# Four residual gemms with rows of tokens out of PSUM, and norms that run one token tile after another

## What is computed

```python
# first block
xn = rms_norm(h, ln1_w); proj = xn @ w_in                      # 1024 -> IN_WIDTH
mix = concat(nsa_mixer(...), retention_mixer(...))
h = h + mix @ w_out                                            # 1024 x 1024
hn = rms_norm(h, ln2_w)
h = h + square(relu(hn @ w_up)) @ w_down                       # 1024 -> 4096 -> 1024
# second block
sh1, sc1, g1, sh2, sc2, g2 = split(silu(c) @ w_ada + b_ada, 6)
hh = standardize(x) * (1 + sc1) + sh1
mix = hybrid_mixer(hh, ...)            # mLSTM and S5, ends in y @ w_mix_out (1024 x 1024)
x = layer_norm(ALPHA * x + (1 + g1) * mix, ln1_gain, ln1_bias)
hh = standardize(x) * (1 + sc2) + sh2
f = conv_glu_ffn(hh, ...)              # 1024 -> 2 x 2816, 2816 -> 1024
x = layer_norm(ALPHA * x + (1 + g2) * f, ln2_gain, ln2_bias)
```

## Time and profile before

| what | us |
|---|---|
| median of the timed runs (3) | 1843.65 (1843.37 to 1845.13) |
| profiled execution, its own time | 1839.39 |
| span of the profiled execution, first to last instruction | 1837.5 |
| PE busy | 1576.4 (86%) |
| DVE busy | 1116.4 (61%) |
| POOL busy | 638.7 (35%) |
| ACT busy | 580.2 (32%) |

### The profile page before, as it was taken

One profiled execution on the slowest core, in us unless ns is written; L12 is line 12 of the kernel. 1 busy time (PEld: TensorE's weight loads), 2 busy tenths in 40 slices (PEclk: granted clock), 3 DMA queues, 4 the chain that ended last, 5 costly groups with the idle time before them and its releaser, 6 DMA issues. The chain is left out here.

```text
span 1837.5 us, 19435 instructions
## 1 busy us (share of the span) xinstructions
PE 1576.4 (86%) x6984; PEld 1225.2 (67%) x6984; DVE 1116.4 (61%) x1935; ACT 580.2 (32%) x779; POOL 638.7 (35%) x456
## 2 busy tenths in 40 slices
PE   3999776788999998979998887566996699999995
PEld 3778534576878777868765554344885588888874
DVE  5743467735777977446899999864644532232236
ACT  3333255214322222233222311354332333333331
POOL 2344000023545554533434241101554244445442
PEclk9999679989999999999999988778998799999998
DMA  6221100042555453222322211122330223222221
GB/s 255 89 74 67 45 1 1 1 176 79 198 173 191 163 195 137 92 92 70 108 97 75 103 69 57 52 78 69 140 115 24 92 99 108 92 92 93 92 90 46
DMA packets 37303, 178.76 MB, mean 97 GB/s; under 512 B 4192, under 2 KB 5088, under 8 KB 22496
## 3 DMA queue, kind: packets, MB, share of 16 engines
q1 hardware_dynamic: 31968, 168.15, 26.3%
q10 hardware_dynamic: 5248, 9.44, 1.4%
HBM read 166.04 MB, written 10.49 MB: 96 GB/s over the span
## 5 line engine op out<-in xcount | busy, mean ns | idle before, releaser
L1132 POOL TENSOR_TENSOR wlo<-raw,whi 128x512 fp32r<-128x512 f32 x336 | 466.2, 1414 | 1157.2 <-ACT whi L753 1157.2
L409 PE MATMUL bank<-Ahi,whi 128*128 128x512 f32 x1152 | 473.8, 411 | 7.9 <-POOL wlo L1134 7.1
L411 PE MATMUL bank<-Ahi,wlo 128*128 128x512 f32 x1152 | 452.5, 393 | 0.0
L410 PE MATMUL bank<-Alo,whi 128*128 128x512 f32 x1152 | 452.3, 393 | 0.0
L409 PEld LDWEIGHTS bank<-Ahi,whi 128*128 128x128 f32 x1152 | 219.2, 190 | 68.2 <-issue 21.6
L410 PEld LDWEIGHTS bank<-Alo,whi 128*128 128x128 f32 x1152 | 218.8, 190 | 54.3 <-issue 10.9
L411 PEld LDWEIGHTS bank<-Ahi,wlo 128*128 128x128 f32 x1152 | 218.3, 189 | 46.7
L409 PE MATMUL bank<-Bhi,whi 128*128 128x512 f32 x560 | 222.9, 398 | 9.3 <-POOL wlo L1134 5.6
L753 ACT ACTIVATE whi<-raw 128x2048 fp32r<-128x2048 f32 x112 | 214.2, 1913 | 52.5 <-DMA raw<-in_ws 44.6
L410 PE MATMUL bank<-Blo,whi 128*128 128x512 f32 x560 | 219.9, 393 | 0.0
L411 PE MATMUL bank<-Bhi,wlo 128*128 128x512 f32 x560 | 219.9, 393 | 0.0
(11 more groups left out here) (366 smaller groups left out, 2047.5 us busy)
## 6 DMA issues: line engine op xcount, KB each, us to landing
raw<-in_ws SPq DMA_DIRECT2D x112, 1024.0 KB, 5.1
adaw<-in_ada SPq DMA_DIRECT2D x48, 512.0 KB, 4.4
spill<-stage ACTq DMA_DIRECT2D x32, 256.0 KB, 2.0
X<-in_x SPq DMA_DIRECT2D x8, 512.0 KB, 5.3
gates<-spill SPq DMA_DIRECT2D x16, 256.0 KB, 5.4
w1k<-in_w1k SPq DMA_DIRECT2D x1, 2048.0 KB, 16.3
w1v<-in_w1v SPq DMA_DIRECT2D x1, 2048.0 KB, 20.5
XM<-spill SPq DMA_DIRECT2D x8, 256.0 KB, 2.9
```

The lines of the kernel that those rows point to most:

```text
L409: pe.matmul(ps[:], wh, hi[:, k], start=(k == 0), stop=False)
L410: pe.matmul(ps[:], wh, lo[:, k], start=False, stop=False)
L411: ins = pe.matmul(ps[:], wl, hi[:, k], start=False, stop=(k == kn - 1))
L1132: pool.tensor_tensor(wlo[slot][:, part], raw[slot][:, part], rd(whi[slot][:, part]), ALU.subtract)
```

## The change

The gemms `wout`, `dn`, `mix` and `fd` now hold the activation tile as the stationary operand and stream 512 weight columns (`token_gemm`). A bank then has 128 tokens by 512 features. Half 0 of the features is made in four T banks, half 1 in G, G, O, O. The number of matmuls stays (192 for 8 feature tiles). Where a norm follows, half 1 runs in the order (part 0, tile 0), (0,1), (0,2), (1,0), (0,3), (1,1), (1,2), then tile 0's transposes (`wout` and `dn3`), then (1,3). DVE adds a bank to `X` directly; ACT copies, sums in `Y` and PE's turns back are gone. For `mix` and `fd` the gain lies along the free dimension: `widen` and `spread` make `G1b` and `G2b` by transposing matmuls, and the addition is two DVE operations.

All norms run tile by tile: root and row scaling on ACT (whole 1024-wide rows of all tiles), then the turned tile is scaled by 8 ACT operations of 128 columns (`scaled`), and DVE splits it (`parts`) after the statistics of the tile behind it. `layer_norm`'s gain and bias are on DVE for all tiles; POOL only makes `wlo`.

Two chunks of zeros (`pad0` after WIN, `pad1` after `if`) make 113 tiles, and move the tile borders: `up0.0` and `up0.1` now share tile 16 (before `up0.0` was the end of tile 15, `up0.1` and `up0.2` tile 16, and so on), `wout.0.0` is the first half of tile 12 (before `wout0` was the end of tile 11). The ada tiles are used one after each `up` chunk of groups 0 to 2, six after the last of them and two between the halves of `dn` (before one after each `up` and `dn` chunk), and the S5 pieces are regrouped. The second load of `GB`, and the weight tiles behind it, now wait for all of the middle LayerNorm.

```diff
     for g, kg in enumerate(FF1_GROUPS):
-        ch += [(f"up{g}.{j}", 8) for j in range(kg)] + [(f"dn{g}.{n}", kg) for n in range(DC)]
-    ch += [(f"us{c}", 8) for c in range(4)] + [("if", 8)]
+        ch += [(f"up{g}.{j}", 8) for j in range(kg)] + token_chunks(f"dn{g}", kg)
+    ch += [(f"us{c}", 8) for c in range(4)] + [("if", 8), ("pad1", 8)]
...
+                def products(ps, q, ks, half, i, k, stop):
+                    b = FIRST_BLOCK[g + 2 * half + q] + 4 * (k - ks[0])
+                    t, c = b // TILE_BLOCKS, b % TILE_BLOCKS
+                    wh, wl = (w[t % 2][:, c * P:(c + 4) * P] for w in (whi, wlo))
+                    h, l = (x[:, k, i * P:(i + 1) * P] for x in (hi, lo))
+                    pe.matmul(ps[:], h, wh, start=(k == 0), stop=False)
+                    pe.matmul(ps[:], h, wl, start=False, stop=False)
+                    return pe.matmul(ps[:], l, wh, start=False, stop=stop)
...
+                    for q, i in ((0, 0), (0, 1), (0, 2), (1, 0), (0, 3), (1, 1), (1, 2)):
+                        run(q, i)
+                    if turns:
+                        normed_tile(s, 0)
+                    run(1, 3)
...
+            def normed_out(s, more=None):
+
+                for i in range(NT + 1):
+                    if i < NT:
+                        root(i, s)
+                        normed_row(i, s)
+                    if i == 1 and more is not None:
+                        hi_upto(more)
+                    if i == 1 and s == 2:
+                        act.wait_ge(sem("mod_ready"), A.due("mod_ready"))
+                    if i:
+                        scaled(i - 1, s)
...
+            def add_token(name, half, i, gain=None, alpha=None):
+
+                n = f"{name}.{half}t{i}"
+                dve.wait_ge(*full(n))
+                ps = bank_of(n)
+                x = X[:, i, half * S:(half + 1) * S]
+                if gain is None:
+                    tt(x, x, ps[:], ALU.add).then_inc(taken(n)[0], 1)
+                    dve.wait_ge(*taken(n))
                 else:
...
+                    t = G8[2]
+                    tt(t[:], ps[:], gain[:, half * S:(half + 1) * S], ALU.mult).then_inc(taken(n)[0], 1)
...
+            def rows_of(name, s):
+
+                for i in range(NT):
+                    add_token(name, 0, i)
+                    half_stats(i, 0)
+                for i in range(NT):
+                    add_token(name, 1, i)
+                    half_stats(i, 1)
+                    row_stats(i, s < 2)
+                    row_scale(i, s < 2)
+                    if i:
+                        parts(s, i - 1)
+                parts(s, NT - 1)
...
                     dve.sem_inc(sem("up_used"), 1)
+                    if g < 3:
+                        ada_tile()
+                if g < 3:
+                    for _ in range(6):
+                        ada_tile()
...
+                for i in range(NT):
+                    add_token(f"dn{g}", 0, i)
+                for _ in range(2):
                     ada_tile()
...
+            for i in range(NT):
+                add_token("mix", 1, i, G1b, ALPHA)
+                half_stats(i, 1)
+                row_stats(i, False)
+                row_scale(i, False)
+                gained(i)
+                half_stats(i, 0)
+                half_stats(i, 1)
+                row_stats(i, False)
+                row_scale(i, False)
+                if i:
+                    parts(3, i - 1)
+            dve.sem_inc(sem("gb_used"), 1)
+            parts(3, NT - 1)
```

More of the change, by code:

```diff
@@ L67, in plan_chunks @@
         ch += [(f"gv{n}", 4), (f"gg{n}", 4), (f"md{n}", 8)]
-    ch += [(f"mix{n}", 8) for n in range(DC)]
+    ch += token_chunks("mix", 8)
     for g, kg in enumerate(FF2_GROUPS):
@@ L428, in _, with spread @@
+            def spread(name, c):
+                pe.wait_ge(sem("mod_wide"), T.due("mod_wide"))
+                ps, where = bank("T")
+                for n in range(4):
+                    ins = pe.matmul(ps[:, n * P:(n + 1) * P], Fb[c % 2][:, n * P:(n + 1) * P], ident, start=True,
+                                    stop=True)
+                done(ins, f"{name}.{c}", where)
             pe.wait_ge(sem("con_in"), T.due("con_in", 16))
-            normed_in(0)
+            for i in range(NT):
+                normed_tile(0, i)
@@ L582, in _ @@
                     done(ins, f"ry{h - 1}", where)
[L585 to L600, removed]
+            token_gemm("wout", Bhi, Blo, 8, "B_ready", True, 1)
             for g, kg in enumerate(FF1_GROUPS):
@@ L802, in _, with plain_rows, through @@
+            def plain_rows(i):
+                root(i, 2)
+                act.wait_ge(sem("rstd_ready"), A.due("rstd_ready"))
+                act.activation(X[:, i, :], X[:, i, :], ACT.Identity, scale=sd[:, i:i + 1],
+                               bias=nmr[:, i:i + 1]).then_inc(sem("ln_rows"), 1)
+            def through(name):
+                for half in range(2):
+                    for q in range(2):
+                        hi_upto(last_tile(INDEX[f"{name}.{half}.{q}"]))
             act.wait_ge(sem("con_in"), A.due("con_in", 16))
@@ L926, in _ @@
                 act.wait_ge(sem("sd_ready"), A.did("sd_ready"))
-            def back_out(name, buf, scale=1.0, wait=None):
-                ps = take(name)
-                if wait is not None:
-                    act.wait_ge(*full(wait))
-                act.activation(buf, ps[:], ACT.Copy, scale=scale).then_inc(taken(name)[0], 1)
-            for n in range(DC):
-                back_out(f"wout{n}", G4[n % 4][:], wait=f"wout{n - 4}T" if n >= 4 else None)
-            sqrt_sd()
-            normed_out(1)
+            through("wout")
+            normed_out(1, last_tile(INDEX["wout.1.1"]) + 1)
             act.wait_ge(sem("cB_in"), A.due("cB_in", 16))
@@ L1093, in _ @@
             act.wait_ge(sem("g8_free"), A.due("g8_free"))
-            for n in range(DC):
-                back_out(f"mix{n}", G8[n % 2][:], scale=mod[:, 16 + n:17 + n],
-                         wait=f"mix{n - 2}T" if n >= 2 else None)
-            sqrt_sd()
-            norm_last_tile()
-            sqrt_sd()
-            normed_out(3)
+            through("mix")
+            for i in range(NT):
+                plain_rows(i)
+                if i == 1:
+                    hi_upto(last_tile(INDEX["mix.1.1"]) + 1)
+                root(i, 3)
+                normed_row(i, 3)
+                if i:
+                    scaled(i - 1, 3)
+            scaled(NT - 1, 3)
             for g, kg in enumerate(FF2_GROUPS):
```

482 lines of the change are left out of this document (244 added, 238 removed).

## The result

The changed kernel is slower: 1933.2 us (median of four runs, 1928.8 to 1936.8) against 1843.5, a ratio of 1.0485 (95% interval 1.0461 to 1.0509). The prediction was 1943 with a range of 1878 to 1975.

A forecast was written before the change was run, and what follows sets the result against it. It took PE's work plus PE's waits as the bound. Terms 57 + 17 + 5 + 10 + 15 - 4 = 100 on the profiled 1839.4 gave 1939.4; with the median 4.3 higher, 1943 us, range 1878 to 1975.

The forecast's parts named there:

- The ring: First FFN, groups 0 to 2: each weight tile's request hangs on the copy of the tile before; +57 us.
- The turn: First FFN: one round from weight copy through ReLU, DVE, request and transfer to the next copy; 16.7 us against PE's 10.9.
- the entry: First FFN, start of each group: the first request is led by three chunks instead of four; 5.5 us more.
- the restart: After a long wait PE runs at the low clock; 2.5 us lost, counted once per first-FFN group.
- the upper of the two bounds: First FFN: DVE runs at its slow pace beside POOL, so a turn takes 16.7 us and the FFN loses 57.
- rival B: First FFN: POOL's pieces lie beside other work, the turn is 13.0 us, the FFN costs 13; total 1899; chance 0.15.
- rival D: First FFN: the low clock holds through the whole ring, not one restart; 25 to 50 us more, total 1980; chance 0.06.
- wout: Gemm wout and its junction: a 7.2 us wait for tile 13 and a longer norm chain; +7 and +10, together +17 us.
- dn3: Junction behind dn3 +7 us, less turns back 3.1, plus tile 0's transposes 1.3; together +5.
- mix: Gemm mix and the junction behind it: tile-by-tile norms make the junction 49.2 us with restart against 39.8; together +10.
- Start: Kernel start to first gemm: norm tile by tile, 48.7 us, 51.2 with the restart, against 36.4; +15.
- Second FFN: Second FFN: waits for Blo (3.5 us) and turns back (3.1) go, tail +1 and spread +1.5; -4.

The follow-up runs named there:

- e1: The changed kernel with SP asking for a first-FFN weight tile behind every even ada load instead of every odd one: 1884.1 us, ratio 1.0225 to the kernel before.
- e2: The changed kernel with DVE using the ada tile ahead of its wait for the chunk's ReLU: 1873.6 us, ratio 1.0172 to the kernel before.
- e3: The changed kernel without DVE's in-place square of the ReLU's result (squaring left out of the computation): 1910.2 us, ratio 1.0363 to the kernel before.

## Why the prediction was right

The sum came close for the reasons it gave. Inside its largest term, though, it shared the loss wrongly between PE's waits and PE's clock; that the total was right all the same was not part of its working.

**The ring: +57 foretold, +52.1 measured over G0 to G2** (334.1 against 282.0). The mechanism is shown by e1, e2 and e3. The turn was put at 16.7 and is 16.0, since the request lands in 6.5 and not 6.8 and DVE's square is 1.33. A group was put at 87.2 + 25.4 = 112.6 and is 110.4, 111.1 and 112.6: its three turns take 48.3, 49.4 and 50.2 together (the first of G1 and of G2 is longer, 17.1 and 17.9) where PE's work is 32.7, so 15.6 to 17.5 are lost in them, and 7 to 8 are left for the entry and the restart, which were put at 5.5 + 2.5. The groups before had lost 20.4 (88.6, 92.0 and 101.4 less 3 x 87.2), not 19.6. That DVE runs at its slow pace in the ring, the upper of the two bounds, was right: all three of its operations behind the copy at 490.54 have the long durations. The lower bound, rival B's 13.0, would have given 1899.

How a group's loss shows itself was wrong. The prediction had PE wait 22.9 us in a group, some 70 in the whole kernel, in stretches of about 6, and lose 2.5 to the clock once. The sums of G0 to G2, first in the changed kernel and then in the one before (the columns as above):

```profile
sum 334.02, PE 287.47 PEld 231.82 DVE 223.40 ACT 66.24 POOL 146.22; mean PE 95.82 PEld 77.27 DVE 74.47 ACT 22.08 POOL 48.74
sum 282.00, PE 269.35 PEld 219.49 DVE 230.95 ACT 80.71 POOL 143.66; mean PE 89.78 PEld 73.16 DVE 76.98 ACT 26.90 POOL 47.89
```

PE is idle for 46.6 us, not 68.7, 45.0 of it in twelve waits of 2.2 to 5.4 for low parts, and busy for 287.5, which is 25.9 more than the 261.6 of its work at full clock, not 7.5. The clock falls again and again, not once in a group: in the 3 us behind ten of the twelve waits it is 0.50 to 0.70 in the mean. Behind the wait that ends at 498.70:

```profile
498.00:503.00 5.00, 4.30 (x10) 3.46 (x11) 4.70 (x7) 0.00 (x0) 0.56 (x1) 0.50 0.43 119
```

That is near to what rival D said, but D added its price to the time, and it isn't added: the turn is set by the request's way round, so a slower PE only waits less in it. The three turns of G0 take 16.0, 16.2 and 16.1 us with waits of 4.94, 2.17 and 3.54. So the group's length could be right while its parts were not.

**wout: +17, measured +13.1** (5.5 in the gemm, 7.6 in the junction), with the clock of the restart, 2.1 in the first chunk, falling into G0. The wait was put at 7.2 and is 7.58. The junction's 22.3 is 21.8; its tile's 7.6 is 7.2.

**dn3: +5, measured +7.5**: 6.4 in the junction, 2.9 in the first chunks of `us` (2.3 of low clock and a wait of 0.57), and -1.8 in G3, which is what the turns back and tile 0's transposes were put at (-3.1 and +1.3). The junction was put at 22.3 and is 23.5.

**mix: +10, measured +6.2** (-2.9, +9.1). The turns back at 7 x 0.44 = 3.1 are the 2.9, and the junction's 46.7 is 46.6. Of the 5.0 more in block 2, 2.9 are dn3's restart and 1.7 are `spread`'s sixteen matmuls (1.5 foretold). For the weight tile that is held until the LayerNorm 2 were counted; PE waits 0.8 for a low part there.

**Start: +15, measured +12.3** (11.1, and 1.2 in the projection): 48.7 foretold, 46.0 measured. Tile 0's splits begin at 25.0 and not 26.4, tile 1's 10.1 later, where 7.5 and 3.7 for the copy and POOL were counted, tile 2's 7.2 behind these; the last part takes 2.5, and 1.2 up to the first product were left out.

**Second FFN: -4, measured -2.7.**

The terms sum to 100, and the two profiled executions differ by 93.5: 88.5 in the terms, 2.1 in the rest of block 2 (`spread`'s 1.7 among them), and 3.0 in attention, which can't be told from its scatter. The medians differ by 89.7. All terms but dn3 and the second FFN were too dear.

What the prediction did not see is the bank: that DVE's S5 pieces, now between the halves of dn, hold PE's banks. It costs up to 10.5 us, but only where the ring is cut (1.5 in the changed kernel), so it hardly showed in the time.

DVE's additions that read a bank kept their pace, as the rule of the Trainium skill (page SBUF — State Buffer, section "Who interferes with whom") has it:

```profile
L1280 DVE TENSOR_TENSOR X<-X,bank 128x512 f32<-128x512 f32 x40 | 27.5, 687 | 58.9 <-PE bank L455 57.8
```

687 ns against the 688 of the earlier trace rows. By their times in the trace only six of the forty have a piece of POOL's work beside them, and these take 0.69 too; of the squares in SBUF (L1721) the fifteen beside such a piece take 1.25 in the mean, the others 0.69.

## What to carry to other kernels

Follow one request all the way round: if what triggers the load of tile m+1 is queued, on any engine, behind an operation that waits for tile m, the stream runs at the sum of its latencies however idle the engines are; moving the trigger ahead by one operation gave back 49 and 60 us here with no instruction added. PE lost its clock in the ring too and the turn got no longer by it, so PE's waits alone (45 us) understate what the ring cost. Cutting a norm into tiles did not shorten it here: one deep lengthened the junctions behind wout and dn3 by 6 to 8 us, and two deep, with the next tile's first steps queued ahead of the last tile's last ones, gave 6 to 7 of them back. And a gemm that leaves its sums in PSUM makes the engine that adds them a holder of banks: whatever is queued ahead of the additions is now in PE's path.

## What the runs showed of the hardware

A DVE operation of 16 columns beside POOL's subtractions takes longer than one of 512 columns alone (0.69). In the changed kernel's S5 pieces (POOL starts a tile's pieces at 571.47):

```profile
571.12 0.17 DVE L1625 TENSOR_TENSOR pw<-s 128x16 f32<-128x16 f32 x1
571.33 0.17 DVE L1627 TENSOR_TENSOR s<-pw 128x16 f32<-128x16 f32 x1
571.54 1.25 DVE L1629 TENSOR_SCALAR pw<-s 128x16 f32<-128x16 f32 x1
572.82 1.21 DVE L1621 TENSOR_TENSOR s<-pw 128x16 f32<-128x16 f32 x1
```

The same two-input operation is 0.18 us alone and 1.21 beside POOL: seven times as long, where the 512-column one is 0.69 and 1.63. The price is near 1 us for each operation at both sizes, so many small operations suffer most. Each of these small ones lasts about as long as one of POOL's pieces beside them (1.29).

The other is how far the attention stage scatters with the clock, 195.5 to 206.1 us over thirteen profiled executions, at granted clocks of 0.83 down to 0.76 with DVE's and ACT's work the same.
